# A transformer trunk: S5's first scan ahead of the memory's norm, relative bias as one matmul, zero matmuls at the start, values in wide columns

## What is computed

```python
h = rms_norm(x, norm_pre_mix)
proj = h @ w_in                                   # S5 | mLSTM | RWKV-7 | MoBA, 256 columns a piece
y_s5 = s5_mixer(u_s5, ...)                        # bu = B u; x_t = a x_{t-1} + bu_t (complex, a scan over time); y = C x
y_ml = mlstm_mixer(p_ml, ...)
y_rw = rwkv7_mixer(p_rw, ...)                     # here: a triangular inverse, built in 6 levels
y_mb = moba_mixer(p_mb, rel_bias)                 # softmax(q k + bias_t[h, t5_bucket(i - j)]) v
x = x + rms_norm(rms_norm_groups(y) @ w_out)
mem_n = rms_norm(mem, norm_mem)
kv = mem_n @ wkv                                  # 1024 columns of keys, 1024 of values
x = x + rms_norm(attention(rms_norm(x) @ wq, kv) @ wo)
gu = rms_norm(x) @ ffn_w_in                       # 2 x 2816 columns
x = x + rms_norm((silu(g) * u) @ ffn_w_out)
```

## Time and profile before

| | us |
|---|---|
| three timed runs | 509.06 median, 508.49 to 510.1 |
| the profiled execution | 507.5 |
| its span | 505.4 |
| PE busy | 483.3 (96%) |
| DVE, ACT, POOL busy | 375.7 (74%), 258.3 (51%), 166.1 (33%) |

### The profile page before, as it was taken

The page is one execution under the profiler, slowest core; times in us unless marked ns, Lnnn a source line. Parts: engine busy times, 40 slices in busy tenths (PEclk is TensorE's granted clock), DMA queues, the critical chain, the costliest instruction groups (busy, mean ns, idle before and its releaser), DMA issues.

```text
span 505.4 us, 9070 instructions
## 1 busy us (share of the span) xinstructions
PE 483.3 (96%) x3770; PEld 438.9 (87%) x3770; DVE 375.7 (74%) x464; ACT 258.3 (51%) x419; POOL 166.1 (33%) x99
## 2 busy tenths in 40 slices
PE   6999899987799899999999999999999999999995
PEld 3999698967699689889999888999999999988884
DVE  3898999996478667689655656799999999962134
ACT  5778784414433145667845747544544444443432
POOL 0004517698956420000000000343344333443460
PEclk9999999979899799999999999999999999999999
DMA  7885238220222202535555260364555455545602
GB/s 261 347 313 182 84 97 320 85 84 1 84 86 84 83 6 103 227 127 207 209 177 199 84 249 10 122 244 167 178 199 206 168 183 208 194 155 190 219 19 83
DMA packets 12692, 78.96 MB, mean 156 GB/s; under 512 B 1483, under 2 KB 2156, under 8 KB 4076
## 3 DMA queue, kind: packets, MB, share of 16 engines
q1 hardware_dynamic: 12652, 78.38, 43.2%
HBM read 76.54 MB, written 1.84 MB: 155 GB/s over the span
## 4 chain that ended last, share of the span: by engine, by line
PE 80%; DVE 10%; ACT 3%; issue 3%; POOL 1%; DMA 1%; SPq 0%; DVEq 0%; ACTq 0%
PE bank L394 79%; DVE we_rest L375 3%; POOL arena L1076 1%; DMA kx<-x_t 1%; ACT we_high L369 1%; DVE bank L1592 1%; DVE arena L1774 1%; DVE arena L1767 1%; DVE arena L1766 1%; DVE wk_rest L375 0%; DVE arena L1645 0%; DVE arena L1662 0%; ACT h_high L1306 0%; ACT arena L1225 0%; PE bank L861 0%
## 5 line engine op out<-in xcount | busy, mean ns | idle before, releaser
L375 POOL TENSOR_TENSOR w_rest<-ring,w_high 128x1024 fp32r<-128x1024 f32 x20 | 48.4, 2420 | 199.2 <-ACT w_high L369 199.2
L394 PE MATMUL bank<-h_high,w_high 128*128 128x256 f32 x384 | 102.9, 283 | 0.0
L369 ACT ACTIVATE w_high<-ring 128x1024 fp32r<-128x1024 f32 x64 | 67.3, 1057 | 69.4 <-PE bank L394 69.3
L394 PE MATMUL bank<-h_rest,w_high 128*128 128x256 f32 x352 | 99.6, 283 | 0.0
L394 PE MATMUL bank<-h_high,w_rest 128*128 128x256 f32 x320 | 90.6, 283 | 0.0
L394 PEld LDWEIGHTS bank<-h_high,w_high 128*128 128x128 f32 x384 | 71.7, 192 | 0.4 <-issue 0.4
L375 DVE TENSOR_TENSOR w_rest<-ring,w_high 128x1024 fp32r<-128x1024 f32 x38 | 48.5, 1283 | 30.1 <-ACT w_high L369 30.1
L394 PEld LDWEIGHTS bank<-h_rest,w_high 128*128 128x128 f32 x352 | 67.6, 192 | 0.0
L394 PEld LDWEIGHTS bank<-h_high,w_rest 128*128 128x128 f32 x320 | 61.4, 192 | 0.0
L394 PE MATMUL bank<-arena 64*64 64x64 f32 (+7 forms) x768 | 46.3, 251 | 3.7 <-ACT arena L1119 1.6
L394 PEld LDWEIGHTS bank<-arena 64*64 64x64 f32 (+4 forms) x768 | 37.8, 143 | 12.5 <-issue 2.8
(11 more groups left out here) (346 smaller groups left out, 1259.8 us busy)
## 6 DMA issues: line engine op xcount, KB each, us to landing
ring<-weights SPq DMA_DIRECT2D x49, 1024.0 KB, 4.8
third_slot<-weights SPq DMA_DIRECT2D x15, 1024.0 KB, 4.8
gain<-gains SPq DMA_DIRECT2D x3, 512.0 KB, 5.9
cst<-consts SPq DMA_DIRECT2D x1, 1216.0 KB, 7.3
par<-params SPq DMA_DIRECT2D x1, 1168.0 KB, 10.4
kx<-x_t SPq DMA_DIRECT2D x2, 512.0 KB, 5.8
ring<-weights SPq DMA_DIRECT2D x2, 512.0 KB, 6.7
vx<-mem_t SPq DMA_DIRECT2D x1, 1024.0 KB, 9.8
```

Source lines behind the costliest of these rows:

```text
L369: nc.scalar.activation(split_half(i)[0], raw_half(i), ACT.Copy).then_inc(S["w_high"], 1)
L375: e.tensor_tensor(rest_, raw_half(i), high.bitcast(F32), ALU.subtract).then_inc(rest_done(i)[0], 1)
L394: return nc.tensor.matmul(out_, lhsT, rhs, start=start, stop=stop, skip_group_check=True)
```

## The change

- PE begins with four matmuls of the zeroed tile `S0_`, as soon as POOL has written the zeros; then comes the relative bias as one matmul (4 weight columns by 384), and nine more matmuls of zeros. ACT empties one bank of four rows for it, where it emptied four of 128, and SP's store to the scratch reads each of the four rows 128 times.
- DVE's `scan(0)` goes ahead of the memory's norm, which moves behind `level_update(2)` and two remainders. POOL's `rotate_back(0)` goes ahead of `level_mask(3)`.
- ACT splits half 24 ahead of the memory's copy, half 25 gets the buffer `w_kx`, and ACT's wait for `rotated_back(1)` moves behind `wkv0`. PE's `s5_in(4)`, `s5_in(5)` and `s5_out(1)` go later, between and behind the two halves of `wkv(0)`.
- DVE's `scan(3)` and `corner` go ahead of `mb_biased`; PE's `corner_t` ahead of `mb_scores`.
- ACT splits halves 12 and 13 ahead of sine and cosine, DVE splits half 12 ahead of the gates' scan.
- The memory's values, and the first pair of the FFN, are computed with matmuls of 512 columns: a half now holds two k-tiles by 512 columns where it held four by 256, and two banks are open together. The banks of q and of some small products are others.

```diff
-            if i < H_WKV:
+            if i < H_WKV or i == H_WKV + 1:
                 return w_mb[i % MID_BUFS]
...
+            def split_wide_values(halves, names, banks, act, parts):
+
+                if 0 in parts:
+                    for name, b in zip(names, banks):
+                        pe_open(pe, name, b)
+                for j in parts:
+                    i = halves[j]
+                    wait_rest(pe, i)
+                    w = [flat(x) for x in split_half(i)]
+                    for m in range(2):
+                        for k in range(2):
+                            kt = 2 * j + k
+                            last = mm3(bank[banks[m]][:, :], [x[:, kt, m * P:(m + 1) * P] for x in act],
+                                       [x[:, 512 * k:512 * (k + 1)] for x in w], kt == 0, kt == KD - 1)
+                        if j == 3:
+                            last.then_inc(full[banks[m]], 1)
...
+            def values_low(*parts):
+                split_wide_values([H_WKV + 8 + j for j in range(4)], ("wkv4", "wkv5"), (1, 7), h_split, parts)
+
+            def values_high(*parts):
+                split_wide_values([2 * S_V6, 2 * S_V6 + 1, H_V7, H_V7 + 1], ("wkv6", "wkv7"), (4, 5), h_split, parts)
...
+            def keep_busy(n):
+
+                for i in range(n):
+                    mm(bank[0][:, 0:256], S0_[:, 0:P], S0_)
+
+            pe.wait_ge(S["zeros_ready"], 1)
+            keep_busy(4)
             pe.wait_ge(S["first_in"], 16)
             pe.wait_ge(S["onehot_in"], 16)
-            for h in range(NH):
-                o = pe_open(pe, f"rel{h}", 4 + h)
-                mm(o[:, 0:384], prm("rel", 33)[:, h:h + 1].to_broadcast([33, P]), const("onehot", 33)).then_inc(full[4 + h], 1)
+            o = pe_open(pe, "rel", 4)
+            mm(o[0:NH, 0:384], prm("rel", 33), const("onehot", 33)).then_inc(full[4], 1)
+            keep_busy(9)
...
             level_x(3, 1)
-            s5_in(4, 2)
-            s5_in(5, 1)
-
             ml_qk(0, 2)
+            wkv(0, 1, (0,))
             ml_qk(1, 0)
             level_p(4, 0, 4)
             level_p(4, 1, 6)
-            wkv(0, 1)
-            s5_out(1, 3)
+            s5_in(4, 5)
+            s5_in(5, 7)
+            wkv(0, 1, (1,))
             level_x(4, 0)
             level_x(4, 1)
+            s5_out(1, 3)
...
             wkv(2, 1)
+            corner_t(0, 4)
+            corner_t(1, 6)
             mb_scores(0, 7)
...
             s5_out(2, 3)
-            corner_t(0, 4)
-            corner_t(1, 6)
...
                 if n == 5:
-                    for h in range(NH):
-                        moved(sp, f"rel{h}")
-                    sp.dma_start(rel_scratch.ap(), E_).then_inc(S["rel_stored"], 16)
+                    moved(sp, "rel")
+                    every_row = bass.AP(rel_scratch, 0, [[384, NH], [NH * 384, P], [1, 384]])
+                    sp.dma_start(every_row, copies(E[0:NH, 0, :], P)).then_inc(S["rel_stored"], 16)
...
             level_mask(2)
+            rotate_back(0)
             level_mask(3)
-            rotate_back(0)
...
-            dve.wait_ge(S["rstd_m"], 1)
-            for k in range(KD):
-                last = v.scalar_tensor_tensor(mem_h[:, k, :], mem_h[:, k, :], prm("norm_mem")[:, k:k + 1], rstd_m,
-                                              ALU.mult, ALU.mult)
-            last.then_inc(S["mem_ready"], 1)
-
+            scan(0)
             rests(H_MID + 3)
             level_update(1)
             rests(H_MID + 4)
-            scan(0)
...
             rests(H_MID + 6)
+            dve.wait_ge(S["rstd_m"], 1)
+            for k in range(KD):
...
+            rests(H_WKV + 1)
+            h_rest(2, mem_h)
+            level_update(3)
             scan(1)
-
-            level_update(3)
-            for j in range(2):
-                h_rest(2 + j, mem_h)
+            h_rest(3, mem_h)
...
             solve_rhs(0)
+            scan(3)
+            corner()
             mb_biased(0)
             mb_biased(1)
             mb_biased(2)
-            scan(3)
             rests(H_WKV + 8)
-            corner()
```

More of the change, by code:

```diff
@@ L821, in _ @@
             attend("mb_o", 2, mbv, PTm)
-            o = pe_open(pe, "mean", 4)
+            o = pe_open(pe, "mean", 6)
             moved(pe, "rw_y")
-            mm(o[:, :], const("pair_ones"), flat(Yrw)).then_inc(full[4], 1)
+            mm(o[:, :], const("pair_ones"), flat(Yrw)).then_inc(full[6], 1)
             o = v3(pe_open(pe, "glu", 3)[:, :], T)
@@ L921, in _, with first_pair @@
                               at_end=lambda: turn_block(0))
[L923 to L928 removed]
+            def first_pair(m, parts):
+                if 0 in parts:
+                    pe_open(pe, f"gu{m}", 4 + m)
                 for j in parts:
[L930 removed]
+                    i = H_FIN + j
                     if m == 0:
                         wait_rest(pe, i)
[L933 to L939 removed]
+                    if j % 2 == 0:
+                        moved(pe, f"fft{2 * m + j // 2}")
+                    w = [flat(x) for x in split_half(i)]
+                    for k in range(2):
+                        kt = 2 * j + k
+                        last = mm3(bank[4 + m][:, :], [x[:, kt, m * P:(m + 1) * P] for x in h_split],
+                                   [x[:, 512 * k:512 * (k + 1)] for x in w], kt == 0, kt == KD - 1)
+                    if m == 1 and j < 3:
                         used(last, i)
[L941 removed]
+                if 3 in parts:
                     last.then_inc(full[4 + m], 1)
                     if m == 1:
[L944 removed]
+                        half_user[H_FIN + 3] = f"gu{m}"
             def turn_first_pair():
@@ L1198, in _ @@
             a.activation(step, prm("log_step"), ACT.Exp).then_inc(S["s5_step"], 1)
-            for h in range(NH):
-                o = wait_full(act, f"rel{h}")
-                a.activation(E[:, h, :], o[:, 0:384], ACT.Copy).then_inc(free_of(f"rel{h}"), 1)
+            o = wait_full(act, "rel")
+            a.activation(E[0:NH, 0, :], o[0:NH, 0:384], ACT.Copy).then_inc(free_of("rel"), 1)
             highs(6)
@@ L1306, in _ @@
                 a.activation(h_split[0][:, ks, :], mem_h[:, ks, :], ACT.Copy).then_inc(S["h_high"], 1)
+            project_values("mb_v", mbv)
+            highs(H_WKV + 2)
             moved(act, "m_row0")
@@ L2259, in _weight_slots @@
     w_out = a["w_out"][0].reshape(KD, P, D)[Y_ORDER]
-    wkv = columns_of(a["xa_wkv"][0])
-    parts += [wkv[:N_WKV], rows_of(w_out), wkv[6:7], columns_of(a["xa_wq"][0]), wkv[7:8], rows_of(a["xa_wo"][0])]
-    gu = columns_of(a["ffn_w_in"][0])
+    w = a["xa_wkv"][0]
+    low, high = wide_columns_of(w[:, D:D + 512]), wide_columns_of(w[:, D + 512:])
+    parts += [columns_of(w[:, :D]), low, rows_of(w_out), high[0:1], columns_of(a["xa_wq"][0]), high[1:2],
+              rows_of(a["xa_wo"][0])]
+    w = a["ffn_w_in"][0]
+    parts.append(wide_columns_of(np.concatenate([w[:, :256], w[:, DFF:DFF + 256]], axis=1)))
+    gu = columns_of(w)
     half = NFF // 2
-    parts.append(np.stack([gu[:half], gu[half:]], axis=1).reshape(2 * half, P, SLOT))
+    parts.append(np.stack([gu[1:half], gu[half + 1:]], axis=1).reshape(2 * half - 2, P, SLOT))
     parts.append(rows_of(a["ffn_w_out"][0]))
```

91 lines of the change are left out of this document (44 added, 47 removed).

## The result

The changed kernel took **524.45 us** (median of four runs, 524.4 to 525.02) where the kernel before took 508.77 on the same chip: ratio 1.0315, 95% interval 1.0289 to 1.0341. It is slower; 497 was forecast. The profiled execution took 524.4, its span 522.3, 16.9 more than before.

A forecast was written before the change was run, and what follows sets the result against it. PE, with 80% of the chain, was the bound, DVE late until about 98 us. Terms -5.1 (to level 5), -1.5 and -2.8 (corner), -1.7 (wide columns) sum to -11.1: 497 us, own range 493 to 500, with rivals 490.5 to 502.

The forecast's parts named there:

- rival 3: Relative bias's store confined to four DMA engines, 7.5 us, delaying slot 6 some 2 us: 500 us; chance 0.10.
- The start: First weight matmuls: the zero fill raises PE's clock, so DVE and all that follows gain 1.2 us.
- The first scan: Up to level_x(3): start's -1.2, PE's wait for rotate_back(0) gone -1.9, clock kept up -3.0; sum -6.1, 112.2 for 118.30.
- From there to level 5: level_x(3) to level 5's product: new 5 us wait for POOL's mask plus 1.4 us of clock; total gain there -5.1.
- rival 4: POOL and DVE collide between second scan and level 5's mask, POOL instructions at 2.6 us or more: slower; chance 0.05.
- The corner: Corner ahead of MoBA's bias: solve_u(0)'s wait goes, -1.5, and the clock stays up, -2.8.
- The wide columns: 144 matmuls of 512 columns in place of 288 of 256: -1.7 us.

The follow-up runs named there:

- the kernel with the store from 128: Changed kernel, but the four bias rows fill 32 partitions each, the store reads 128 partitions, and three zero matmuls follow in place of nine: 503.58 us, ratio 0.9895.

## Why the prediction was wrong, by its own steps

**The step that failed is the cost of the relative bias's store: nothing in the sum, 3 us in rival 3, and 20.9 measured (524.45 against 503.58).** The rival had the place right: a store with four rows outermost, slot 6 behind it, its rounding late. It counted engines and nothing else: four of 16, each at a sixteenth of 418 GB/s, so 104 GB/s and 7.5 us, slot 6 2 us late, 500. As a price of four engines that was right. With partitions 0, 36, 72 and 108 the store ran at 101 GB/s on as few engines, and that cost nothing (503.7). What the count left out was the way out of SBUF: from partitions 0 to 3 the store ran at 24 to 25 GB/s in all and took 31 us, and PE lost 18.35 us in one wait and part of its clock behind it. The rule of the Trainium skill that the prediction weighed ("DMA: Bandwidth & Descriptors", Rules for kernel authors) holds in the shares: 0.21 for four rows, 0.44 for eight. The term that was missing stands in the port table of the Trainium skill ("SBUF — State Buffer", The DMA port swizzle), with which the four rates agree. The prediction's rows could not show it: the earlier trace rows gave a landing time behind another transfer, not a rate.

**The start**, -1.2: the size was near, the cause in doubt. DVE was 0.86 earlier in the changed kernel, and 1.89 in the kernel with the store from 128, whose shorter fill ended ahead of the weights. But without any fill it was 0.86 earlier as well (22.80), so the changed kernel's fourteen matmuls, which ended at 12 and not at 10, had no part in it that the runs show. What else in the start brings the 0.86 was not settled.

**The first scan**, -6.1 at `level_x(3)`: right. The changed kernel gained 5.1 between `s5_out(0)`'s wait and there (it stood 19.95 us later than before at the start of `mb_k`, ahead of the readout, and 14.87 at `level_x(3)`), and with the store repaired `level_x(3)` began 5.6 us earlier than before.

**From there to level 5**, -5.1: wrong by 3.7, the second failure. The wait came as forecast (5.49 and 5.44 for 5), with half a clock behind it. Not seen was that the norm, behind two remainders, would run beside POOL's rotation: 7.06 us for 3.24. The prediction took 3.24 from a place where POOL was idle. Its rival 4 had that collision, on POOL's instructions alone. DVE was late for PE twice, and its second scan, for which POOL waits, stood at 119.0 to 121.4, where 119 was forecast for its end. Putting the norm back took the two waits away and made another at 93.35, so the norm's place alone is not worth the 3.7. Level 5's product ended 1.4 us earlier than before, not 5.1. Behind it, from 154 to 162 us, the clock fell a second time with PE busy throughout, where it had been up before, and `wkv(2)` ended 1.1 later than before. The stretch, of the kernel before and of the one with the store from 128:

```profile
154.00:162.00 8.00, 8.00 (x71) 7.54 (x71) 7.36 (x7) 2.65 (x5) 5.68 (x5) 1.00 0.36 131
```

```profile
154.00:162.00 8.00, 8.00 (x60) 7.57 (x60) 6.52 (x6) 2.33 (x5) 5.27 (x4) 0.79 0.31 125
```

From -5.1 to +1.1 are 6.2 of the 6.6 us between 497 and 503.6. Why the clock fell there stays open.

**The corner**, -4.3: right, 14.6 us to 10.4 for the stage in the changed kernel; undoing it gave the stage 14.7 again and cost the whole 2.6 to 3.5 us. **The wide columns**, -1.7: 1.35 (offset +18.26 to +16.9 at the end), by the traces alone; no run undid them.

The range had no room for this. Both its ends came from waits on engines. The one edit that touched a DMA was priced by its engines alone, and by the prediction's own words no row showed what it would do.

## What to carry to other kernels

A store that reads a few neighbouring partitions is as slow as the narrow way out there, 24 GB/s from partitions 0 to 3, and the weights queued behind it pay. Before a copy over 128 partitions is dropped as waste, price the transfer by its partitions, and spread even four rows over the tile. Price a moved vector instruction at both speeds, with GpSimd idle and busy beside it. A stall removed is worth what the next wait leaves of it: here four variants that took waits of 1.7 to 5.4 us away ended within 1.6 us of one another.

## What the runs showed that was not expected

- The rate of a store depends on which partitions it reads: 24 GB/s from 0 to 3, 49 from 0 to 7, 98 from eight at steps of 16, 101 from four at steps of 36.
- A slow store on another queue still delays the weights, 9.02 us in place of 22.39.
- The same waits did not always end in the same clock. Behind 0.80 and 1.44 us of idle the 24 matmuls at 117.91 took 4.6 us in the kernel with the store from 128; behind 0.81 and 1.44 us, at 119.09, they took 3.1 in the one with level 5's mask first.
- The same fill at the start took two lengths. Its last three matmuls, six pieces, take 2.93 or 1.56 us; where they are short, PE then stands 3.3 us, and the pitch of the weight matmuls goes from 0.12 to 0.21 about 1 us after they begin. `x_scale` of the first product comes at 22.80 to 23.06 in the four traces with the short one, as without a fill (22.80), and at 21.77 at the earliest with the long one. The fill's 1.0 us is there in some executions and not in others. PE's rows in two kernels with the same start, the store from 128 and the corner ahead of `scan(3)`:

```profile
6.23 2.93 PE L394 MATMUL bank<-arena 128*128 128x256 f32 x6
10.45 0.38 PE L394 MATMUL bank<-h_high,we_high 128*128 128x256 f32 x1 [1.30 <-DVE we_rest L375]
```

```profile
5.57 1.56 PE L394 MATMUL bank<-arena 128*128 128x256 f32 x6
10.46 0.39 PE L394 MATMUL bank<-h_high,we_high 128*128 128x256 f32 x1 [3.33 <-DVE we_rest L375]
```
